# Two fused transformer blocks: product with values a step later in the last layers, gates in odd steps, third spatial sum ahead of the maximum, mask of the forgetting attention added by VectorE

## Chip, core and metric

The kernel runs on one core of one Trainium2 chip. The metric is the time of the program on the device in microseconds. Three runs of the kernel before gave 1648.83, 1653.23 and 1654.64; their median is 1653.23.

## The reference

512 tokens of width 1024, everything in float32. A first block of two layers (a convolution with memory attention, then forgetting attention with memory attention, each followed by a gated feed-forward net with a short convolution) feeds a second block of two layers, the "last layers". What the change touches is the forgetting attention and the two last layers:

```python
# forgetting attention, 12 heads of 64, block of 128 queries
logits = einsum("bqhd,bkhd->bhqk", qb, kb) * scale
logits = logits + cum_logf[:, :, q0:kend, None] - cum_logf[:, :, None, :kend]
logits = where(kpos[None, :] <= qpos[:, None], logits, -inf)
p = softmax(logits, axis=-1)
out = einsum("bhqk,bkhd->bqhd", p, vb)

# a last layer
proj = einsum('bsd,de->bse', rmsnorm(x), w_in[l])
u_a, v_a, g_a, q, k, v, g_b = split(proj)
z = einsum('hij,bcjhd->bcihd', spatial_w, layernorm(v_a)) + spatial_b
y_a = u_a * z * silu(g_a)
y_b = attention(rope(norm(q)), rope(norm(k)), v) * silu(g_b)   # 8 heads, 2 of keys and values
x = x + rmsnorm(concat([y_a, y_b]) @ w_out[l]) * post_g
```

## The kernel before

All activations stay on the chip. Each weight tile of 1024x128 is a "unit": SP loads it (raw), ScalarE rounds it to w_hi, GpSimd (POOL) subtracts for w_lo, and TensorE computes 8 tiles k of three matmuls of 512 columns each (L1886 to L1888) into one of two accumulators. VectorE scales the result out of PSUM (L1214), which frees the accumulator for the unit after the next. Every engine's program is written out by hand in its own block, in the order in which it issues; semaphores tie them together. An engine that waits holds up all that is queued behind the wait.

Attention is cut into steps that are set between the tiles of the units (the argument `before` of `unit`: a list of tile number and action). In a last layer of 22 units, `steps_in(j)` gives the steps of unit j: one every 6 tiles from unit 9 on, 18 in all for 16 blocks (a pair of heads and 128 queries each; 4 blocks make a pair of heads in full). In step i:

- TensorE computes the scores of block i into one of two pairs of banks (L2068, L2069), and, if `batch_weighed(i)` names one, the product of a batch of two blocks with the values (`weigh`, L2445).
- VectorE takes the maxima (`maxima`, L1333 to L1335), turns the probabilities of batch `batch_turned(i)` in 32x32 blocks (`turned_probs`, L1724; the single buffer pt_c must have been read by the product before), takes the reciprocals (`inverses`, L1346), and multiplies a finished pair of heads by its gate (`gated`, L1731). The product of an even batch reuses the single output bank and waits for that gate (yb_ok).
- ScalarE computes the exponentials (L801), GpSimd scales them (L662), and SP exchanges quarters of a batch by 16 DMAs (L627) ahead of the transposes.

Between these lie, in order: queries and keys with their rotation (`rope`, `q_low`, `key_norm`, `k_low`) in units 4 to 8; the layer norm of the spatial path (`add_square`, row sums L2031, normalization on ScalarE L1052); transposes to tokens (`to_tokens`, L2414) in units 16 and 17; four spatial sums (`spatial`, L2425) around units 18 and 19, each into the one bank b_mix, so that each waits until VectorE has mixed the one before (`mixed`, L1737 and L1738). After unit 21 `token_output` runs the output projection tile by tile, with the product of the last batch ahead of tile 4. In layer 0 TensorE also transposes x between the tiles of units 8 and 9 (L2400).

In the forgetting attention (24 blocks of 128 queries with 128, 256, 384 or 512 keys, between the tiles of the units that make keys and values) there is one pair of score banks (`spaced`). For each of two heads TensorE adds to the scores the gate row (L2078) and the triangle of the mask, as a bf16 identity times a bf16 mask (L2082); the maximum on VectorE is L1338, the exponentials L809, the scaling L662, the transposes L2091, the product L2108. The next block's scores wait for the exponentials of this one (at_exp).

Of the kernel before, what the change touches and what calls it, by code (L numbers as in the profile page):

```python
# [19 lines left out]
P = 128  # L20
# [16 lines left out]
QT = T // P  # L37
# [97 lines left out]
def two_blocks(nc, wstream, xT, memT, params, consts, rope, wsT, sbT, post_rows, out):  # L135
# [8 lines left out]
    with ctx:  # L144
# [52 lines left out]
        row_m = put("row_m", [P, 1], f32)  # L197
        row_t = put("row_t", [P, 1], f32)
        row_r = put("row_r", [P, 2 * QT], f32)
        ident_b = put("ident_b", [P, P], bf16)  # L200
        mask_b = put("mask_b", [P, P], bf16)
        sel = put("sel", [P, N_FOX], f32r)
        h0 = cursor[0] + (xs_at - cursor[0]) % LINE

# [312 lines left out]

        def batch_weighed(s):

            return (s - 5) // 2 if s % 2 == 1 and s >= 5 else None  # L520

        def swaps(l, batch):

# [200 lines left out]
        def _(act):  # L724
# [169 lines left out]
            high(6)  # L894
            act.wait_ge(params_in, 16)
            act.wait_ge(consts_in, 16)
            A(ident_b[:], ident, ACT.Copy).then_inc(consts_b, 1)
            A(mask_b[:], mask, ACT.Copy).then_inc(consts_b, 1)
            A(sel[:], gate_of, ACT.Copy).then_inc(consts_b, 1)
            for u in range(7, U_GLU + AHEAD):  # L900
                high(u)
# [296 lines left out]
        def _(dve):  # L1198
# [125 lines left out]
            def maxima(a, i):  # L1324
                nk = keys_of(a, i % QT)
                b = a.i0 + i
                n = 2 * (b % 2)
                dve.wait_ge(at_s, 2 * (b + 1))
                if b >= 2:
                    dve.wait_ge(at_exp, 2 * (b - 1))  # L1330
                scores_of = a.s[b % len(a.s)][:, :, 0:nk]
                if a.scale_rows:
                    own.link(V.tensor_reduce(nraw[:], scores_of, AX.X, ALU.max, negate=True))  # L1333
                    V.tensor_scalar(nmax[:, n:n + 1], nraw[:, 0:1], head_r[:, 2 * i:2 * i + 1], None, MUL)
                    V.tensor_scalar(nmax[:, n + 1:n + 2], nraw[:, 1:2], head_r[:, 2 * i + 1:2 * i + 2], None,  # L1335
                                    MUL).then_inc(at_max, 1)
                else:
                    V.tensor_reduce(nmax[:, n:n + 2], scores_of, AX.X, ALU.max, negate=True).then_inc(at_max, 1)  # L1338

            def inverses(a, i):  # L1340
# [312 lines left out]
            for l in range(2):  # L1653
# [95 lines left out]
                for j in range(IN2_UNITS):  # L1749
                    if l == 0 and j == 3:  # L1750
                        final_norm()
                    if j == 10:
                        va_sum(3)
                    if j == 19:
                        mixed(1)
                    if j == 20:
                        mixed(3)
                    for n, (_, i) in enumerate(steps_in(j)):
                        if j == 18 and n == 1:
                            mixed(0)  # L1760
                        if i < a.n:
                            maxima(a, i)
                        batch = batch_turned(i)
                        if batch is not None:
                            turned_probs(batch)
                        if j == 13:
                            invert(f"ln{l}")
                        if j == 19:
                            mixed(2)
                        if i < a.n:  # L1770
                            inverses(a, i)
                        if j == 9 and n == 0:
                            va_sum(1)
                            va_sum(2)
                        if j == 12 and n == 0:
                            for t in (2, 3):
                                add_square(f"ln{l}", t)
                        if i >= 8 and i % QT == 0:
                            gated(i // QT - 2)
                        if i == a.n + 1:  # L1780
                            for k in range(AT - 1):
                                y_low(k, gb[:, k, :])
                    if j == 4:
                        rope(0)
                    if j == 5:
                        rope(1)
                        rope(2)
                    if j == 6:
                        rope(3)
                        invert(f"qk{l}")  # L1790
                        rope(4)
                        q_low(0)
                    if j == 8:
                        k_low()
                    if j == 7:
                        key_norm()
                    if j in (10, 13, 16):
                        q_low((10, 13, 16).index(j) + 1)
                    if j == 10:
                        for t in (0, 1):  # L1800
                            centred(t)
                    if j == 11:
                        for t in (2, 3):
                            centred(t)
                        for t in (0, 1):
                            add_square(f"ln{l}", t)
                    if j == 14:
                        dve.wait_ge(cast_up, cast_no[f"ln{l}"] + 1)
                        for t in range(AT):
                            V.tensor_tensor(va[:, t, :], va[:, t, :], cast_bank(f"ln{l}")[:],  # L1810
                                            MUL).then_inc(s_norm if t < AT - 1 else cast_down, 1)
                    if j >= 20:
                        ya(j - 20)
                        dve.wait_ge(ya_ok, AT * l + j - 19)
                    dst = (qk[:, j, :] if j < 5 else vch[:] if j == 5 else va[:, j - 6, :] if j < 10
                           else gb[:, j - 10, :] if j < 14 else ua[:, j - 14, :] if j < 18 else ga[:, j % 2, :])
                    if j == 5:
                        values_scaled(u0 + j)
                    else:
                        scaled(dst, u0 + j, bank=b_s[2] if j == 2 else None)  # L1820
                ya(2)
                for t in range(2):
                    y_low(AT - 1 + t, ua[:, t, :])
                turned_probs(a.n // 2 - 1)
# [56 lines left out]
        def _(pe):  # L1881
# [176 lines left out]
            def scores(a, i):  # L2058
# [17 lines left out]
                if a.causal:  # L2076
                    for e in range(2):
                        MM(dst[:, e, 0:nk], sel[half(e), 2 * p + e:2 * p + e + 1].to_broadcast([HD, P]),  # L2078
                           a.gates[half(e), 0:nk], start=False, stop=False)

                    for e in range(2):
                        MM(dst[:, e, nk - P:nk], ident_b[:], mask_b[:], start=False, stop=True).then_inc(at_s, 1)  # L2082

            def transposes(a, i):
                b = a.i0 + i
# [231 lines left out]
            def b_step(i):  # L2317
                if i < B_BLOCKS:
# [2 lines left out]
                        pe.wait_ge(acc_free, accs_before(U_B) + Q_UNIT)  # L2321
                    if a is att_f and n == 0:
                        pe.wait_ge(f_done, 2)
                        pe.wait_ge(consts_b, 3)
                    if a is att_f and n % QT == 0:
                        pe.wait_ge(acc_free, accs_before(U_B) + K_UNIT[n // QT] + 1)
                    scores(a, n)
# [31 lines left out]
            for l in range(2):  # L2359
# [87 lines left out]
                                last.then_inc(at_o, 1)  # L2447

                def attention_step(i):
                    if i == 0:  # L2450
                        pe.wait_ge(vt_down, VT_C0 + l + 1)
                    if i < a.n:
                        if i % QT == 0:
# [10 lines left out]
                for j in range(3, IN2_UNITS):  # L2464
# [22 lines left out]
                    if j == 19:  # L2487
                        spatial(3)
                token_output(l, u0 + IN2_UNITS, a0 + IN2_UNITS, KT * (SP_YC0, SP_YC1)[l],
                             before=[(4, lambda: weigh(a.n // 2 - 1))])  # L2490

# [141 lines left out]
```

## Time and profile before

| | |
|---|---|
| median of three runs | 1653.23 us |
| the profiled execution | 1653.36 us, of it 1651.6 span |
| TensorE busy | 1605.1 us (97%), 8452 matmuls |
| VectorE busy | 883.3 us (53%) |
| ScalarE busy | 733.1 us (44%) |
| GpSimd busy | 714.2 us (43%) |
| granted TensorE clock, mean | 0.996 |
| chain that ended last | TensorE 85%, VectorE 10%, ScalarE 2%, issue 2% |

The trace is of one execution. A row of the order of time reads: start and duration in us, engine, line of the kernel, operation, written and read tensors, shape, count of merged instructions, and in brackets how long the engine had stood idle before it and what released it. PE is TensorE, DVE VectorE, ACT ScalarE, POOL GpSimd. The forgetting attention runs from 656 to 777 us, the last layer 0 from about 1200 to 1430, the last layer 1 from there to the end.

### The profile page before, as it was taken

Reading aid. Unit: us, or ns where it says so; the run is one execution under the profiler, and the core shown is the slowest. Engines: PE = TensorE matmul, PEld = TensorE weight load, DVE = VectorE, ACT = ScalarE, POOL = GpSimd, SP = SyncE. Lnnn points to the kernel's source line nnn. Section 1 sums busy time; section 2 is a strip of 40 time slices with the busy share of each in tenths; the row PEclk is TensorE's granted clock in tenths of the full one; section 3 lists DMA queues with packets and bytes.
Section 4 is the critical chain, followed back from the end, with each engine's and each line's share of the span. In section 5 each row is a group of like instructions: output and inputs, shape, how many; then the busy total and the mean of one; then the engine's idle time right before and its main releaser. Section 6 shows DMA issues by size and latency. Waiting matters only on the chain.

```text
span 1651.6 us, 23637 instructions
## 1 busy us (share of the span) xinstructions
PE 1605.1 (97%) x8452; PEld 1270.7 (77%) x8452; DVE 883.3 (53%) x1451; ACT 733.1 (44%) x1157; POOL 714.2 (43%) x406
## 2 busy tenths in 40 slices
PE   8899999999999999999999999999999999999998
PEld 7656788888888887666888888888887777887776
DVE  7887545445521124434366666611286654587654
ACT  6433544444432235444455555533335643535532
POOL 4433334444445444443444444454435542445431
PEclk9999999999999999999999999999999999999999
DMA  7212133323333332111223233333422443324441
GB/s 255 65 52 65 53 101 102 99 89 91 102 113 102 103 103 71 47 50 39 90 90 102 90 90 100 102 115 112 136 77 81 135 135 109 121 65 131 126 139 51
DMA packets 52972, 161.01 MB, mean 97 GB/s; under 512 B 8736, under 2 KB 8864, under 8 KB 52896
## 3 DMA queue, kind: packets, MB, share of 16 engines
q1 hardware_dynamic: 51744, 156.31, 30.9%
q10 hardware_dynamic: 1152, 3.67, 0.7%
q8 instruction: 49, 0.80, 0.2%
q14 instruction: 27, 0.22, 0.0%
HBM read 141.08 MB, written 2.10 MB: 87 GB/s over the span
## 4 chain that ended last, share of the span: by engine, by line
PE 85%; DVE 10%; ACT 2%; issue 2%; DMA 0%; POOL 0%; DVEq 0%; SPq 0%; ACTq 0%; POOLq 0%
PE banks L1886 23%; PE banks L1888 23%; PE banks L1887 23%; PE banks L2445 2%; PE banks L1932 2%; PE banks L1933 2%; PE banks L1934 2%; PE banks L2161 1%; PE banks L2073 1%; PE banks L2108 1%; DVE roped L1678 1%; PE banks L2091 1%; DVE chain L1497 1%; DVE pt_c L1724 1%; PE banks L2068 1%
## 5 line engine op out<-in xcount | busy, mean ns | idle before, releaser
L651 POOL TENSOR_TENSOR w_lo<-raw,w_hi 128x1024 fp32r<-128x1024 f32 x252 | 610.1, 2430 | 700.4 <-ACT w_hi L734 700.2
L1886 PE MATMUL banks<-xs_hi,w_hi 128*128 128x512 f32 (+2 forms) x1488 | 590.7, 397 | 5.1 <-DVE xs_lo L1559 1.6
L1888 PE MATMUL banks<-xs_hi,w_lo 128*128 128x512 f32 (+2 forms) x1488 | 577.5, 388 | 0.0
L1887 PE MATMUL banks<-xs_lo,w_hi 128*128 128x512 f32 (+2 forms) x1488 | 576.6, 388 | 0.0
L734 ACT ACTIVATE w_hi<-raw 128x1024 fp32r<-128x1024 f32 x255 | 263.8, 1052 | 235.8 <-PE banks L1888 204.6
L1886 PEld LDWEIGHTS banks<-xs_hi,w_hi 128*128 128x128 f32 x1488 | 280.2, 188 | 74.4 <-issue 19.0
L1888 PEld LDWEIGHTS banks<-xs_hi,w_lo 128*128 128x128 f32 x1488 | 280.0, 188 | 57.8
L1887 PEld LDWEIGHTS banks<-xs_lo,w_hi 128*128 128x128 f32 x1488 | 280.6, 189 | 52.3 <-issue 0.5
L1886 PE MATMUL banks<-hid_hi,w_hi 128*128 128x512 f32 x352 | 136.9, 389 | 0.0
L1887 PE MATMUL banks<-hid_lo,w_hi 128*128 128x512 f32 x352 | 136.9, 389 | 0.0
L1888 PE MATMUL banks<-hid_hi,w_lo 128*128 128x512 f32 x352 | 136.9, 389 | 0.0
L1410 DVE TENSOR_TENSOR x<-x,banks 128x512 f32<-128x512 f32 x16 | 11.0, 688 | 182.4 <-PE banks L1888 182.4
L1384 DVE TENSOR_TENSOR u_v<-banks,rstd 128x512 f32<-128x512 f32 x44 | 30.5, 692 | 127.5 <-PE banks L1888 127.5
L662 POOL TENSOR_SCALAR prob_c<-prob_c,rinv 128x512 f32<-128x512 f32 x64 | 53.3, 845 | 91.2 <-DVE rinv L1346 91.2
L801 ACT ACTIVATE prob_c<-banks,nmax,head_r 128x512 f32<-128x512 f32 x64 | 49.3, 774 | 89.4 <-DVE nmax L1335 89.3
L662 POOL TENSOR_SCALAR prob<-prob,rinv 128x256 f32<-128x256 f32 (+3 forms) x80 | 44.0, 563 | 88.1 <-DVE rinv L1346 87.9
L851 ACT ACTIVATE t_v<-u_v,par 128x512 f32<-128x512 f32 x44 | 35.9, 816 | 102.7 <-DVE u_v L1384 102.7
L809 ACT ACTIVATE prob<-banks,nmax 128x256 f32<-128x256 f32 (+3 forms) x80 | 39.8, 502 | 88.0 <-DVE nmax L1338 87.7
L1886 PEld LDWEIGHTS banks<-hid_hi,w_hi 128*128 128x128 f32 x352 | 66.1, 188 | 13.8
L1888 PEld LDWEIGHTS banks<-hid_hi,w_lo 128*128 128x128 f32 x352 | 66.1, 188 | 13.7
L1887 PEld LDWEIGHTS banks<-hid_lo,w_hi 128*128 128x128 f32 x352 | 66.1, 188 | 13.6
L856 ACT ACTIVATE hid_hi<-t_g 128x512 f32 x44 | 27.8, 632 | 80.6 <-DVE t_g L1397 80.6
(273 smaller groups left out, 2018.9 us busy)
## 6 DMA issues: line engine op xcount, KB each, us to landing
raw<-wstream SPq DMA_DIRECT2D x255, 512.0 KB, 3.5
swap_c<-prob_c SPq DMA_DIRECT2D x256, 64.0 KB, 2.0
x<-xT SPq DMA_DIRECT2D x4, 512.0 KB, 9.7
out<-pt SPq DMA_DIRECT2D x8, 256.0 KB, 2.0
memx<-memT SPq DMA_DIRECT2D x4, 256.0 KB, 5.1
ws_sb<-wsT ACTq DMA_DIRECT2D x2, 512.0 KB, 4.6
rope_sb<-rope ACTq DMA_DIRECT2D x2, 512.0 KB, 6.1
qk<-post_rows ACTq DMA_DIRECT2D x2, 512.0 KB, 5.0
```

The costliest lines, as they stand in the source:

```text
L651: nc.gpsimd.tensor_tensor(w_lo[s][:].rearrange("p k c -> p (k c)"), raw[s][:], w_hi[s][:].rearrange("p k c -> p (k c)").bitcast(f32), SUB) ...
L662: nc.gpsimd.tensor_scalar(p, p, rinv[:, n:n + 1], 1.0, MUL, MUL).then_inc(at_p, 1)
L734: A(w_hi[s][:].rearrange("p k c -> p (k c)"), raw[s][:], ACT.Copy).then_inc(unit_hi, 1)
L801: A(probs_of(i // 2)[:, :, 2 * (i % 2) + e, :], a.s[b % len(a.s)][:, e, :].rearrange("p (c k) -> p c k", k=P), ACT.Exp, bias=nmax[:, n:n + 1],
L809: A(prob[b % 2][:, e, 0:nk], a.s[b % len(a.s)][:, e, 0:nk], ACT.Exp, bias=nmax[:, n:n + 1], accum_out=rsum[:, n:n + 1]).then_inc(at_exp, 1)
L851: A(dst[:], src[:, 2:T + 2], ACT.Identity, scale=par[:, bass.ds(ch * 3 + (w0 + 2), 1)], bias=par[:, bass.ds(ch + b0, 1)]).then_inc(tap0, 1)
L1886: MM(dst, w_hi[slot][:, k, :], hi, start=start, stop=False)
L1887: MM(dst, w_hi[slot][:, k, :], lo, start=False, stop=False)
L1888: return MM(dst, w_lo[slot][:, k, :], hi, start=False, stop=stop)
L1932: MM(dst, hi, w_rows(w_hi, slot, half), start=start, stop=False)
L1933: MM(dst, lo, w_rows(w_hi, slot, half), start=False, stop=False)
L1934: return MM(dst, hi, w_rows(w_lo, slot, half), start=False, stop=stop)
```

## The change

- The mask is no longer multiplied in on TensorE. VectorE adds it, from the constants in float32, to the last 128 key columns of both heads' scores in PSUM, ahead of the maximum, and waits for its own add. The two bf16 copies of identity and mask, made by ScalarE at the start, go.
- `batch_weighed` gives even steps from 6 on: each product with values is one step (6 tiles) later. Batch 6, which was in step 17, stands ahead of tile 1 of the output projection; batch 7 stays ahead of tile 4.
- `gated` stands in steps 9, 13 and 17 instead of 8, 12 and 16.
- `mixed(2)` stands ahead of the maximum and the transposes of step 14 (unit 19) instead of behind them.
- TensorE waits for the turned values (vt_down) at step 1 instead of step 0.
- `q_low(0)` stands behind the scaling of unit 6 instead of ahead of it.
- `y_low(2)` stands behind `ya(2)` after the last unit instead of with y_low(0) and y_low(1) in step 17.

```diff
-            return (s - 5) // 2 if s % 2 == 1 and s >= 5 else None
+            return s // 2 - 3 if s % 2 == 0 and s >= 6 else None
...
-            A(ident_b[:], ident, ACT.Copy).then_inc(consts_b, 1)
-            A(mask_b[:], mask, ACT.Copy).then_inc(consts_b, 1)
...
                 else:
+                    if a.causal:
+                        diagonal = a.s[b % len(a.s)][:, :, nk - P:nk]
+                        own.link(V.tensor_tensor(diagonal, diagonal, mask.unsqueeze(1).to_broadcast([P, 2, P]), ADD))
                     V.tensor_reduce(nmax[:, n:n + 2], scores_of, AX.X, ALU.max, negate=True).then_inc(at_max, 1)
...
+                        if j == 19:
+                            mixed(2)
                         if i < a.n:
                             maxima(a, i)
...
-                        if j == 19:
-                            mixed(2)
                         if i < a.n:
                             inverses(a, i)
...
-                        if i >= 8 and i % QT == 0:
+                        if i >= 9 and i % QT == 1:
                             gated(i // QT - 2)
                         if i == a.n + 1:
-                            for k in range(AT - 1):
+                            for k in range(2):
                                 y_low(k, gb[:, k, :])
...
-                        q_low(0)
...
                         scaled(dst, u0 + j, bank=b_s[2] if j == 2 else None)
+                    if j == 6:
+                        q_low(0)
                 ya(2)
+                y_low(2, gb[:, 2, :])
...
                            a.gates[half(e), 0:nk], start=False, stop=False)
-
-                    for e in range(2):
-                        MM(dst[:, e, nk - P:nk], ident_b[:], mask_b[:], start=False, stop=True).then_inc(at_s, 1)
+                           a.gates[half(e), 0:nk], start=False, stop=True).then_inc(at_s, 1)
...
-                    if i == 0:
+                    if i == 1:
                         pe.wait_ge(vt_down, VT_C0 + l + 1)
...
-                             before=[(4, lambda: weigh(a.n // 2 - 1))])
+                             before=[(1, lambda: weigh(a.n // 2 - 2)), (4, lambda: weigh(a.n // 2 - 1))])
```

## Rows read from the trace of the kernel before

**Rows 1.** The page, part 1: busy us, share of the span, instructions.

```profile
PE 1605.1 (97%) x8452; PEld 1270.7 (77%) x8452; DVE 883.3 (53%) x1451; ACT 733.1 (44%) x1157; POOL 714.2 (43%) x406
```

**Rows 2.** Waits of TensorE, whole span: us in total, times, longest.

```profile
PE banks L2425 <- DVE ua L1738: 5.1, 2, 2.6
PE banks L2445 <- DVE gb L1731: 4.4, 2, 2.2
...
PE banks L2445 <- DVE pt_c L1724: 3.5, 2, 1.7
PE banks L2068 <- issue: 1.9, 1, 1.9
...
PE banks L1886 <- DVE va L1214: 1.2, 2, 0.6
...
PE banks L2068 <- DVE k_lo L1697: 0.5, 1, 0.5
```

**Rows 3.** Windows of 10 us: engines' busy time, granted clock, DMA share, GB/s.

```profile
1350.00:1360.00 10.00, 10.00 (x48) 7.39 (x47) 3.50 (x8) 5.11 (x9) 2.75 (x3) 0.89 0.36 120
1530.00:1540.00 10.00, 7.81 (x36) 5.44 (x35) 6.93 (x13) 7.18 (x14) 4.36 (x5) 0.83 0.41 100
1580.00:1590.00 10.00, 10.00 (x50) 7.15 (x47) 3.34 (x7) 3.80 (x7) 4.53 (x5) 0.83 0.34 113
```

**Rows 4.** Order of time, ScalarE, layer 0, around the first scores.

```profile
1246.08 0.60 ACT L832 ACTIVATE vtok<-banks 128x512 f32<-128x512 f32 x1
```

**Rows 5.** Order of time, TensorE, layer 0, steps 5 to 15.

```profile
1277.52 1.95 PE L2445 MATMUL banks<-pt_c,vtok 128*64 128x256 f32 x16 [1.73 <-DVE pt_c L1724]
...
1282.26 0.95 PE L2031 MATMUL banks<-cst,sq_sum 128*128 128x1 f32 x8
...
1305.34 1.95 PE L2445 MATMUL banks<-pt_c,vtok 128*64 128x256 f32 x16 [2.19 <-DVE gb L1731]
...
1309.39 0.60 PE L2414 MATMUL banks<-cst,va 128*128 128x128 f32 x4
...
1331.62 0.39 PE L2068 MATMUL banks<-k_hi,q_stack 128*128 128x512 f32 x1
...
1339.37 1.09 PE L2425 MATMUL banks<-ws_sb,va_tok 128*64 128x128 f32 x16
...
1347.55 1.09 PE L2425 MATMUL banks<-ws_sb,va_tok 128*64 128x128 f32 x16 [2.56 <-DVE ua L1738]
```

**Rows 6.** The same stretch of TensorE in layer 1: product of batch 2.

```profile
1535.48 2.77 PE L2445 MATMUL banks<-pt_c,vtok 128*64 128x256 f32 x16 [2.19 <-DVE gb L1731]
...
1541.14 0.60 PE L2414 MATMUL banks<-cst,va 128*128 128x128 f32 x4
```

**Rows 7.** Order of time, VectorE and ScalarE, layer 0.

```profile
1277.43 1.77 DVE L1238 TENSOR_TENSOR sq_sum<-sq_sum,sq_qk 128x512 f32<-128x512 f32 x2
...
1303.84 2.92 ACT L1052 ACTIVATE va<-va,par 128x512 f32<-128x512 f32 x4
...
1330.32 0.67 DVE L1731 TENSOR_TENSOR gb<-banks,gb 128x512 f32<-128x512 f32 x1
...
1336.02 0.17 DVE L1346 RECIPROCAL rinv<-rsum 128x2 f32<-128x2 f32 x1 [1.70 <-ACT prob_c L801]
```

**Rows 8.** Forgetting attention around a block of 256 keys; two VectorE groups (ns, or us).

```profile
684.42 0.29 PE L2082 MATMUL banks<-mask_b,ident_b 128*128 128x128 bf16 x2
684.54 0.39 PE L2091 MATMUL banks<-cst,prob 128*128 128x128 f32 x2
...
686.29 0.20 ACT L809 ACTIVATION_READ_ACCUMULATOR prob<-banks,nmax 128x1 f32 x1
...
686.93 0.92 PE L2073 MATMUL banks<-kf,qf 64*128 64x384 f32 x4
...
L1440 DVE TENSOR_TENSOR mem_kv<-banks,rstd_m x8: 406/412/425, 38.0 to 180.9; 128x256 f32<-128x256 f32 x8
...
L1678 DVE TENSOR_TENSOR roped<-roped,rope_sb 128x512 f32<-128x512 f32 x10 | 17.3, 1733 | 0.3
```

More of the change, by code:

```diff
@@ L199, in two_blocks @@
         row_r = put("row_r", [P, 2 * QT], f32)
-        ident_b = put("ident_b", [P, P], bf16)
-        mask_b = put("mask_b", [P, P], bf16)
         sel = put("sel", [P, N_FOX], f32r)
@@ L2078, in scores @@
                         MM(dst[:, e, 0:nk], sel[half(e), 2 * p + e:2 * p + e + 1].to_broadcast([HD, P]),
-                           a.gates[half(e), 0:nk], start=False, stop=False)
-                    for e in range(2):
-                        MM(dst[:, e, nk - P:nk], ident_b[:], mask_b[:], start=False, stop=True).then_inc(at_s, 1)
+                           a.gates[half(e), 0:nk], start=False, stop=True).then_inc(at_s, 1)
             def transposes(a, i):
@@ L2323, in b_step @@
                         pe.wait_ge(f_done, 2)
-                        pe.wait_ge(consts_b, 3)
+                        pe.wait_ge(consts_b, 1)
                     if a is att_f and n % QT == 0:
```

## The prediction

> **What bounds the kernel.** I read the page first, then TensorE's waits, the clock by windows, and last the order of time on TensorE, VectorE and ScalarE around each wait. TensorE is busy for 1605.1 of 1651.6 us [rows 1], so an edit pays only if it takes instructions off TensorE or shortens one of its waits. The waits that the change touches are few and large [rows 2]: third spatial sum 5.1 us in two, product with values behind the gate 4.4 in two, behind turned probabilities 3.5 in two, first scores 1.9 once, unit 8 of each layer 1.2 in two, first scores behind k_lo 0.5 once. In the last two layers the clock falls too: 0.89 of full speed after the spatial wait of layer 0, 0.83 after the gate wait and 0.83 after the spatial wait of layer 1 [rows 3]. That is a stay at 1.2 GHz instead of 2.4 in part of each window. Both idles of 2.56 us and one of the two of 2.19 led to it; 1.93 and 1.73 did not.
>
> **What is removed in the last layers.** (a) The wait for the turned values moves from step 0 to step 1. It held step 0 for 1.93 us: ScalarE copied vtok until 1246.68 [rows 4] and the scores began right after. k_lo, the next release, was there before TensorE came (TensorE waits for it in layer 1 only). Gain 1.93, layer 0 only; in layer 1 the same scores wait 0.5 us for k_lo [rows 2], which does not move. (b) The product of batch 0 waited 1.73 us for the transposes of its own step [rows 5]; one step later these have ended. Gain 1.73 per layer. (c) The product of batch 2 waited 2.19 us for the gate of pair 0, queued on VectorE behind a transpose [rows 5]. The gate now stands in odd steps and the product in the next even step, over 4 us later. Gain 2.19 per layer. (d) The fourth spatial sum waited 2.56 us for the third one's mixing, queued behind the maximum and the transposes of step 14 [rows 5]; now it is ahead of both. Gain 2.56 per layer. (e) q_low(0) moves behind the scaling of unit 6, which ends the 0.6 us before unit 8. I give it nothing: key_norm, k_high and k_lo follow at their old times, and the next wait (first scores on k_lo in layer 1, the turned x tiles in layer 0) grows by the same 0.6. Sum a to d: 1.93 + 2 x (1.73 + 2.19 + 2.56) = 14.9 us.
>
> (f) Clock. From the product of batch 2 to the next transposes layer 1 took 1541.14 - 1535.48 = 5.66 us, layer 0 at full clock 1309.39 - 1305.34 = 4.05 [rows 5, 6]. A fall costs 1.6 us. There are three, each behind a wait that goes: 4.8 us.
>
> **What is late next.** These are the new waits, worked out by laying the new order over the old rows.
> (g) Row sums of the layer norm. Without wait and product of batch 0, TensorE reaches them 1.73 + 1.95 less 0.08 of overlap, plus a little issue time, some 3.76 us earlier: 1282.26 - 3.76 = 1278.50. VectorE finishes the squares at 1277.43 + 1.77 = 1279.20 [rows 5, 7]. New wait 0.75 per layer.
> (h) The first tokens (1309.39) need ScalarE's normalization, which ended at 1303.84 + 2.92 = 1306.76 [rows 5, 7]. TensorE comes 1.73 + 2.19 + 1.9 (one product less by then) - 0.75 = 5.1 earlier, at 1304.3. The normalization hangs on VectorE and ScalarE; by my estimate it moves 1.9 earlier (VectorE idled about 2.5 us for the scores of block 6, and ScalarE's exponentials of that block, held by their table loads, leave 1.9 of it), so it ends at 1304.85. New wait about 0.6 per layer (0 to 2.4).
> (i) The product that stood in step 13 (1.95) is gone from there, and the gate of pair 1 (0.6 net of overlap) stands in front of the mixing of the second spatial sum. From the scores of block 13 (1331.62) the reciprocal comes after 4.40 us (1336.02), then gate 0.7, scaling 0.6, mixing 1.43: end at +7.2. TensorE is ready for the third spatial sum at 1339.37 - 1331.62 - 1.97 = +5.78 [rows 5, 7]. New wait 1.4 per layer, bounds 0.8 (the gate overlaps) to 2.0.
> Sum g to i: 2 x (0.75 + 0.6 + 1.43) = 5.6 us.
> The tail: VectorE's transposes of batch b now wait for the product of b-1 in the same step, 0.4 us behind the maximum, and are needed two steps on. Queued behind them are the reciprocal, the next scaling and POOL's probabilities; none is within 1 us of a use. The swap DMAs on SP start at their old distance from the scores (10 to 11 us of issue per batch) and land before each transpose; batch 7 lands some 1 us late for VectorE, but 5 us ahead of TensorE. The product of batch 6 in tile 1 of the output projection needs nothing late; y_low(2) is ready about 5 us before tile 2. Cost nothing; if that cover went, the 1 to 5 us would have to be used up first.
>
> **Forgetting attention.** 24 blocks lose two mask matmuls: 684.54 - 684.42 = 0.12 us to the next start [rows 8], 24 x 0.12 = 2.9. VectorE gets an add over 128x256 with a PSUM input and output. The nearest row, PSUM times SBUF at that size, takes 0.41 [rows 8]; the upper bound is the 128x512 gate product of 0.67 [rows 7]. The trace shows no such add in place at 256 columns. With 0.03 to the dependent reduction it is 0.45, and the scores are reported 0.22 earlier without the mask. The maximum ends 0.23 later. Behind it wait exponentials, reciprocal, POOL, transposes, and, as there is one score bank pair, the next block's scores. Tightest are 256 keys before 384: exponentials end 686.49 with the read at 686.29, next scores 686.93 [rows 8], 0.44 free against 0.23 + 0.12. Where POOL comes late already, 0.12 to 0.24 of the gain is given back (three blocks, 0.6), and the last block lies open on both (0.35). Net 2.9 - 1.0 = 1.9 us, bounds 0 (add of 0.67) to 3.3 (0.21 at the five outputs, no loss). The two copies removed at the start lie on ScalarE where TensorE waits for nothing of theirs; nothing.
>
> One question decides whether that price holds: VectorE's adds on roped, both inputs in SBUF, average 1.73 us at 128x512 against 0.67 for the gate product [rows 7, 8]. If the mask add were stretched alike it would cost 1 us or more. The stretched rows have two SBUF inputs, the unstretched a PSUM one; the mask add is of the second kind.
> The Trainium skill, page SBUF — State Buffer, section Who interferes with whom, says the same: a VectorE instruction with two SBUF inputs contends with a GpSimd instruction that reads SBUF, one with at most one does not. By that rule the add keeps its 0.41 and the sum below stands; were the inputs' place of no account, the sum would be that of R5.
>
> **Sum.** 14.9 + 4.8 - 5.6 + 1.9 = 16.0. The profiled execution took 1653.36 (1651.6 of span, 1.8 around it), 0.1 above the median 1653.23. 1653.36 - 16.0 = 1637.4 us.
>
> **Rivals.**
> R1, forecast, 1637.4, chance 0.54; its own range 1635 to 1640.
> R2, no new waits: VectorE and ScalarE follow as fast as TensorE. Then 14.9 + 4.8 + 1.9 = 21.6: 1631.8. For it: VectorE idles 1.7 us before many reciprocals. Against: in g and i those idles are already counted. 0.15.
> R3, clock: the new 1.4 us waits, or their sum with those before, bring the falls back. Two falls 3.2: 1640.6; three 4.8: 1642.2. For it: at 2.19 us it went both ways. Against: nothing at 1.93 or less did. 0.16.
> R4, the attention chain eats the mask's gain: add of 0.67 plus a longer link, so the four tight blocks and the last lose 0.3 each and POOL's more: 1639.4. 0.08.
> R5, slower: the mask add is stretched as the roped ones are. Extra time x per block first fills 0.1 (before 384), 0.5 (before 512) and 1.3 (before 256) and then stands on TensorE: six pairs, 6 x (3x - 1.9) from x = 1.3 on. It outweighs 16.0 at x = 1.5; at x = 1.8, as in the longest roped adds, it is 21, and the time 1658. Against: every row with a PSUM input. 0.02.
> That the reorder does not move what it says (the product still waits in its new step) is a case too: b and c stay with their clock fall, 9.4 us back, 1646.8; against it are the 4 us margins. 0.05.
>
> **Range and chances.** R1, R2, R3 and R4 hold 0.93; between 1631.5 and 1642.5 lie nearly all of them. A measurement of this kernel can tell about 0.3% (5 us) from no change: faster means under 1648.3. Faster 0.93, same 0.05, slower 0.02.
>
> **What would show it.** Right: no TensorE wait on the gate or the transposes before products with values; the first scores of layer 0 right behind the products before them; VectorE's mask add near 0.41 us; new waits of TensorE on sq_sum (0.75), va (0.6) and ua at the third spatial sum (1.4), each twice; windows at clock 1.00 throughout both layers; TensorE's wait on POOL in the attention up by under 1 us. Wrong: the wait at the third spatial sum at 2 us or more with a clock under 1.00 behind it; a mask add over 0.7 us; waits on the scores (exponentials) in the attention.

## The result and the profile after

The changed kernel takes 1638.13 us (median of 4, 1637.64 to 1638.63) against 1653.27 for the kernel before in the same session (median of 4): ratio 0.991, 95% interval 0.9896 to 0.9923. The forecast was 1637.4, from 16.0 us of gain. The profiled execution took 1638.61 with a span of 1636.8, so the span fell by 14.8 us.

The page, part 1 (busy us, share of the span, instructions), answers to [rows 1]:

```profile
PE 1599.8 (98%) x8404; PEld 1266.5 (77%) x8404; DVE 895.1 (55%) x1475; ACT 730.7 (45%) x1155; POOL 713.4 (44%) x406
```

TensorE lost 5.3 us of busy time and the span lost 14.8, so nearly two thirds of the gain is idle time. VectorE gained 24 instructions and 11.8 us, which costs the span nothing by itself.

TensorE's waits over the whole span (us in total, times, longest), which answer to [rows 2]:

```profile
PE banks L2423 <- DVE ua L1737: 2.9, 2, 1.4
...
PE banks L2032 <- DVE sq_sum L1234: 1.5, 2, 0.7
...
PE banks L2069 <- DVE k_lo L1696: 1.3, 1, 1.3
PE banks L2412 <- ACT va L1048: 1.3, 2, 0.7
...
PE banks L2398 <- DVE banks L1684: 0.4, 1, 0.4
...
PE banks L2398 <- ACT x L1073: 0.4, 1, 0.4
```

The four large rows of before have no successor: no product with values waits, neither for the gate nor for turned probabilities, and the first scores of layer 0 don't either. What was 14.9 us of waits is gone. In their place stand the third spatial sum (2.9), the row sums (1.5) and the first tokens (1.3): 5.7 where 5.6 was forecast.

The same places in order of time on TensorE, layer 0 (answers to [rows 5]; start us, us, engine, line, operation, with the idle time before it and its releaser in brackets):

```profile
1275.93 1.05 PE L2032 MATMUL banks<-cst,sq_sum 128*128 128x1 f32 x8 [0.74 <-DVE sq_sum L1234]
...
1279.34 1.95 PE L2443 MATMUL banks<-pt_c,vtok 128*64 128x256 f32 x16
...
1301.68 0.66 PE L2412 MATMUL banks<-cst,va 128*128 128x128 f32 x4 [0.60 <-ACT va L1048]
...
1305.26 1.95 PE L2443 MATMUL banks<-pt_c,vtok 128*64 128x256 f32 x16
...
1333.29 1.09 PE L2423 MATMUL banks<-ws_sb,va_tok 128*64 128x128 f32 x16 [1.44 <-DVE ua L1737]
...
1340.95 1.09 PE L2423 MATMUL banks<-ws_sb,va_tok 128*64 128x128 f32 x16
```

The new waits are 0.74, 0.60 and 1.44 us; the forecast had 0.75, 0.6 and 1.4. The fourth spatial sum (1340.95) waits no longer. The windows (length, busy times, granted clock third from the right) answer to [rows 3]:

```profile
60.00:70.00 10.00, 7.66 (x33) 5.06 (x31) 8.42 (x17) 4.23 (x12) 3.34 (x5) 0.83 0.16 52
...
1350.00:1360.00 10.00, 10.00 (x54) 7.55 (x52) 8.95 (x13) 6.81 (x11) 3.17 (x2) 1.00 0.55 148
1530.00:1540.00 10.00, 10.00 (x54) 7.45 (x53) 7.99 (x12) 8.10 (x13) 7.04 (x5) 1.00 0.61 152
1580.00:1590.00 10.00, 10.00 (x53) 7.52 (x52) 6.98 (x10) 3.20 (x5) 2.38 (x1) 1.00 0.54 157
```

Both last layers run at 2.4 GHz as long as TensorE works. One new stay at 1.2 GHz lies in 60 to 70 us, beside the first memory attention, where TensorE also waits.

Where in the span the time went is read from the first and last start of two lines of the code (times of least, median and longest in ns, then first and last start). The first line below is the scores of the forgetting attention, the second the head sums in unit 6 of both last layers (first of layer 0, last of layer 1), in the kernel before and then in the changed one:

```profile
L2073 PE MATMUL banks<-kf,qf x96: 272/481/693, 662.1 to 766.7; 64*128 64x128 f32 x24, 64*128 64x256 f32 x24, 64*128 64x384 f32 x24, 64*128 64x512 f32 x24
L2371 PE MATMUL banks<-cst,sq_qk x80: 165/251/251, 1219.8 to 1462.6; 128*128 128x2 f32 x80
```

```profile
L2074 PE MATMUL banks<-kf,qf x96: 271/482/694, 662.7 to 765.3; 64*128 64x128 f32 x24, 64*128 64x256 f32 x24, 64*128 64x384 f32 x24, 64*128 64x512 f32 x24
L2369 PE MATMUL banks<-cst,sq_qk x80: 165/251/252, 1218.7 to 1454.4; 128*128 128x2 f32 x80
```

These two lines cut every kernel of this study into three stretches: A from the first forgetting scores to the head sums of layer 0 (the attention, with a feed-forward stage that doesn't change), B from there to the head sums of layer 1 (most of layer 0), C from there to the end of the span. The table below is read in that way from each trace, which is of one execution; the last column is the median of all. The time ahead of A is left out: it differs by up to 1.2 us from one execution to the next, as the first transfers land.

```
kernel              A      B      C     median us
before            557.7  242.8  189.0   1653.3
changed           556.0  235.7  182.4   1638.1
mask_only         556.0  242.9  189.0   1651.9
values_wait_only  557.6  240.6  189.0   1651.3
mixing_only       557.6  238.7  183.1   1644.7
products_only     557.6  238.3  182.9   1643.1
mixing_back       556.1  236.7  183.5   1640.8
qlow_back         556.1  235.7  182.4   1638.1
gates_even        556.0  235.1  181.9   1637.0
mixing_early      556.0  234.2  181.0   1635.3
three_moved       556.0  233.6  180.2   1633.5
tokens_later      556.0  233.1  179.7   1632.6
mask_twice        558.9  235.7  182.5   1641.8
mask_sbuf         572.1  235.7  182.5   1654.9
```

The changed kernel gains 1.7 in A (forecast 1.9), 7.1 in B and 6.6 in C. The forecast's terms for layer 0 are 1.93 + 1.73 + 2.19 + 2.56 + one clock fall of 1.6 - 2.75 of new waits = 7.3, for layer 1 1.73 + 2.19 + 2.56 + 3.2 - 2.75 = 6.9. Some 0.6 of the 15.4 went in a later start of A (662.7 against 662.1), which belongs to no edit.

### The profile page after: what moved, and what is told of

Same layout as the page of the kernel before. It is cut to its first block, busy times and chain, and to the rows that moved or that the text cites. A ratio compares the mean times of both kernels' runs of the same rounds, so it can differ in the third digit from the quotient of the medians.

```text
span 1636.8 us, 23565 instructions
## 1 busy us (share of the span) xinstructions
PE 1599.8 (98%) x8404; PEld 1266.5 (77%) x8404; DVE 895.1 (55%) x1475; ACT 730.7 (45%) x1155; POOL 713.4 (44%) x406
## 4 chain that ended last, share of the span: by engine, by line
PE 81%; DVE 9%; SPq 3%; ACT 3%; issue 2%; DMA 1%; POOL 1%; DVEq 0%; ACTq 0%; POOLq 0%
PE banks L1887 22%; PE banks L1889 22%; PE banks L1888 22%; SPq L625 3%; PE banks L1933 2%; PE banks L1934 2%; PE banks L1935 2%; PE banks L2159 1%; PE banks L2074 1%; PE banks L2089 1%; PE banks L2106 1%; PE banks L2443 1%; DVE roped L1677 1%; DVE chain L1496 1%; ACT prob_c L799 1%
```

## The experiments

Kernels of one session share their runs of the kernel before (medians 1653.83, 1653.72, 1653.57 and 1653.47 in the four sessions).

### The parts alone, on the kernel before

**mask_only.** The forgetting attention's part alone.

```diff
-                        MM(dst[:, e, nk - P:nk], ident_b[:], mask_b[:], start=False, stop=True).then_inc(at_s, 1)
...
+                        own.link(V.tensor_tensor(diagonal, diagonal, mask.unsqueeze(1).to_broadcast([P, 2, P]), ADD))
```

> The kernel before with the forgetting attention's part alone: 48 mask matmuls go, VectorE adds the mask in PSUM. Forecast: 1.9 us less than before (0 to 3.3), about 1651.4; mask add 0.43 us, TensorE's wait for POOL in that attention up by less than 1 us, nothing changed in the last layers and their three clock falls still there. R4 (the attention's chain eats the gain): within 0.2 us of before, TensorE's waits up by as much as the matmuls saved. R5 (add stretched to 1.8 us): 21 us slower, about 1674.

Measured 1651.91, ratio 0.9988 (0.9979 to 0.9998). Stretch A took 556.0 us, 1.7 less, and B and C did not move. TensorE waited 1.3 us for POOL in that attention instead of 0.9, and for nothing else there that it had not waited for before. R4 and R5 are out.

**values_wait_only.** The wait for the turned values in step 1.

```diff
-                    if i == 0:
+                    if i == 1:
                         pe.wait_ge(vt_down, VT_C0 + l + 1)
```

> The kernel before with the wait for the turned values in step 1 instead of step 0, and nothing else. Forecast: 1.9 us less, layer 0 only, about 1651.4: the first scores of layer 0 start right behind the product before them, and layer 1 keeps its 0.5 for k_lo. Rival (k_lo or step 1 is late next): under 0.5 less.

Measured 1651.32, ratio 0.9979 (0.997 to 0.9989). B is 2.2 shorter, C unchanged, and the row of 1.9 us is gone. The size is right, but the clock did something that the forecast's reading does not allow. Everything from there on in layer 0 runs 2 us earlier and is otherwise the same; its waits of 2.19 and 2.56 us are both still there:

```profile
1303.17 2.47 PE L2445 MATMUL banks<-pt_c,vtok 128*64 128x256 f32 x16 [2.19 <-DVE gb L1731]
...
1347.00 1.09 PE L2425 MATMUL banks<-ws_sb,va_tok 128*64 128x128 f32 x16 [2.56 <-DVE ua L1738]
```

and its windows:

```profile
1300.00:1310.00 10.00, 7.81 (x38) 5.46 (x37) 5.35 (x10) 8.80 (x16) 3.27 (x5) 0.83 0.48 121
1340.00:1350.00 10.00, 7.44 (x44) 5.81 (x45) 7.17 (x11) 2.57 (x5) 2.89 (x3) 1.00 0.42 96
1350.00:1360.00 10.00, 10.00 (x52) 7.53 (x51) 5.54 (x9) 6.69 (x11) 4.25 (x4) 1.00 0.47 158
```

The fall now follows the 2.19 us (in the kernel before that stretch was at full clock: the product took 1.95 [rows 5], here 2.47), and none follows the 2.56, where before one did [rows 3]. The same two idles, 2 us earlier in time, changed places.

Whether the 2 us did this is not shown, since there is one trace of each kernel and the executions of one kernel differ by as much as the falls are worth. Two of the ten of this kernel took 1646.34 and 1647.62 us at a mean granted clock of 0.998, the other eight 1650.28 to 1652.88 at 0.994 to 0.996. Of the 52 executions of the kernel before that this study has, two took 1648.49 and 1648.83, the others 1652.01 to 1656.13. The 5 us are the size of the three falls (4.8), so these few executions may well have had none; no trace was taken of them.

**mixing_only.** The mixing of the third spatial sum ahead of the maximum.

```diff
+                        if j == 19:
+                            mixed(2)
                         if i < a.n:
                             maxima(a, i)
...
-                        if j == 19:
-                            mixed(2)
```

> The kernel before with the third spatial sum's mixing ahead of the maximum and the transposes of its step, and nothing else. By the forecast's terms: both waits of 2.56 before the fourth spatial sum go, and with them the clock falls behind them (2 x 1.6): 8.3 us less than before, about 1645.0, windows behind 1350 and 1580 at full clock, the one behind 1530 still low. If the clock falls have another cause than that wait: 5.1 less, about 1648.2, with the falls still in the windows. If something else of that step is late next: 1653.

Measured 1644.69, ratio 0.9941 (0.9925 to 0.9958). B is 4.1 shorter (2.56 + 1.6 makes 4.2). C is 5.9 shorter, where 2.56 + 1.6 is only 4.2: the fall behind the gate in layer 1, which was to stay, went too. Its wait did not:

```profile
1531.65 1.95 PE L2445 MATMUL banks<-pt_c,vtok 128*64 128x256 f32 x16 [2.19 <-DVE gb L1731]
```

and the window behind it was at full clock:

```profile
1530.00:1540.00 10.00, 8.35 (x46) 6.66 (x47) 4.51 (x9) 7.36 (x14) 5.11 (x5) 1.00 0.48 122
```

This is the same idle of 2.19 us, with 1.95 us for the product behind it instead of 2.77 in [rows 6]. Total 5.1 + 4.8 = 9.9 against 10.0 in B and C. So in this trace all three falls are gone and were worth 1.6 each, but they do not belong each to its own wait. The traced execution was the shortest of the four (1643.69 us at a mean clock of 0.999); the others took 1644.30 to 1645.28 at 0.996. In the two longest of them the fall behind the gate may have stayed, as I had expected; that is not shown.

**products_only.** The products with values one step later, on the kernel before.

```diff
-            return (s - 5) // 2 if s % 2 == 1 and s >= 5 else None
+            return s // 2 - 3 if s % 2 == 0 and s >= 6 else None
...
-                             before=[(4, lambda: weigh(a.n // 2 - 1))])
+                             before=[(1, lambda: weigh(a.n // 2 - 2)), (4, lambda: weigh(a.n // 2 - 1))])
```

> The kernel before with the products with values one step later and nothing else; gates stay in even steps, the fourth spatial sum stays behind the maximum. By the forecast's terms: the waits for transposes (2 x 1.73) and for the gate (2 x 2.19) go, and one clock fall behind the gate in layer 1 (1.6): 9.4. New: row sums 2 x 0.75, tokens 2 x 0.6, third spatial sum 2 x 0.75, and the fourth waits 2.9 in place of 2.56 (its transposes now wait for a product): 4.9. Net 4.5, about 1648.8, with clock falls behind the two fourth spatial sums left. R2 (no new waits): 1643.9. The reorder doesn't do what it says: about 1653, with products still waiting.

Measured 1643.12, ratio 0.9931 (0.9914 to 0.9947): 5.7 below what I expected, and the only one of the four times that I had wrong. The waits for the gate and for turned probabilities are gone. What I had wrong is the fourth spatial sum:

```profile
1345.18 1.09 PE L2425 MATMUL banks<-ws_sb,va_tok 128*64 128x128 f32 x16 [0.94 <-DVE ua L1738]
```

It waits 0.94 us, not 2.9. The product of batch 4 now stands in step 14, between the third sum and the fourth, and its own 1.95 us cover the wait: 2.56 + 0.4 - 1.95 = 1.0. I had moved the product and had not moved its length. That makes 3.9 in two layers. The clock is full in both layers, which makes another 3.2. With these 7.1 the expected 4.5 become 11.6; B and C are 10.6 shorter, and the 1.0 between is not explained. The new wait of 0.9 for a weight tile in this trace lies at 13.75 us, ahead of stretch A, where the start differs from one execution to the next.

The parts therefore don't add: products alone 10.7, mixing alone 9.1, mask 1.9, values 2.5, together 24.2, while the change gives 15.7 against the same 1653.8 (15.1 in its own session). The stretches of the traces show where the excess lies: the parts give 10.6 + 10.0 + 1.7 + 2.2 = 24.5 there, and the change 15.4. Of the 9.1 too many, 4.8 are the clock falls, which either of the first two takes away whole in its trace, and 3.2 are the wait of the fourth sum, which either shortens (2 x 1.62 by the products, and again in the whole 2 x 2.56 of the mixing). The last 1.1 is the price of the gates in odd steps, which only the whole change pays: in products_only the third sum waits 0.8 us, in the change 1.44 (see gates_even).

### Parts taken back from the changed kernel

**mixing_back.** The reverse of mixing_only's edit.

> The changed kernel (1638.1) with the third spatial sum's mixing put back behind the maximum and the transposes of its step. By the forecast's terms: the fourth spatial sum waits 2.56 again in each layer, and 0.4 more as its transposes now wait for a product: 2 x 2.9 = 5.8, and two clock falls of 1.6 come back: 9.0 slower, about 1647.1. If an idle of that length does not bring the falls: 1643.9 with full clock in both layers.

Measured 1640.79, ratio 0.992 (0.9903 to 0.9936), 2.7 above the changed kernel and 6.3 below what I expected. The fourth sum waits again, for 0.94 us in either layer, and B and C grow by 1.0 and 1.1. It is the same 1.0 as in products_only, and no fall comes with it. So within this change the third part is worth 2 to 3 us, not the 5.1 and two falls that the prediction wrote beside it; the credit was right for the sum only.

**qlow_back.** The first remainder of the queries back in front of the scaling of unit 6.

> The changed kernel with the first remainder of the queries back in front of the scaling of unit 6. Forecast (term e, worth nothing): within 0.3 us of the changed kernel, 1638.1: 0.6 comes back before unit 8 in each layer and 0.6 goes from the waits behind it (k_lo in layer 1, x tiles in layer 0). Rival (it is worth its 1.2): 1639.3.

Measured 1638.08, ratio 0.9905 (0.9888 to 0.9921). A, B and C are those of the changed kernel within 0.1. TensorE waits 1.1 us before unit 8 again, and k_lo holds it for 0.4 instead of 1.3. Term e is worth nothing, as forecast.

**gates_even.** The gates back in even steps.

```diff
-                        if i >= 9 and i % QT == 1:
+                        if i >= 8 and i % QT == 0:
```

> The changed kernel (1638.1) with the gates back in even steps, products still one step later. The prediction's term i put 0.6 of the third spatial sum's 1.4 down to the gate of pair 1 in front of the second mixing. If so, that wait falls to about 0.8 in both layers (the gate then stands in 1.5 us in which VectorE waits for the first spatial sum), and the time to about 1636.9. Rival: the gate in even steps is late for something else there (the product of batch 2 waits for it again, as before the change): 1638 to 1642.

Measured 1637.0, ratio 0.9902 (0.9888 to 0.9917): 1.1 faster than the change. The third spatial sum waits 0.8 us instead of 1.44. The gate in an odd step is what put 0.6 of that wait there in each layer, and nothing needed it: with the products a step later the even step is early enough. This part of the change costs 1.1 us.

### The new waits taken away

**mixing_early.** In the changed kernel VectorE idles 1.69 us before the reciprocal of block 13, and the second spatial sum ends in that time. Its mixing goes there:

```diff
-                    if j == 19:
-                        mixed(1)
...
+                        if j == 18 and n == 1:
+                            mixed(1)
                         if i < a.n:
                             inverses(a, i)
```

> The changed kernel with the second spatial sum's mixing moved ahead of the reciprocal of block 13, into 1.7 us in which VectorE waits for the exponentials; the gate of pair 1 and the scaling then stand behind it. If that gate and the reciprocal in front of the mixing are what the third spatial sum waits for (term i): its wait of 1.44 goes in both layers, 2.9 us less, about 1635.2. Rival: the reciprocal and scaling, now 0.5 and 1.4 us later, are late next (accumulator of unit 20, batch 6): under 1 us gained.

Measured 1635.25, ratio 0.9886 (0.987 to 0.9903): 2.9 less, as expected. VectorE in order of time, layer 0, of the changed kernel and then of this one:

```profile
1330.54 0.17 DVE L1345 RECIPROCAL rinv<-rsum 128x2 f32<-128x2 f32 x1 [1.69 <-ACT prob_c L799]
1330.62 0.69 DVE L1730 TENSOR_TENSOR gb<-banks,gb 128x512 f32<-128x512 f32 x1
1331.22 0.68 DVE L1210 TENSOR_TENSOR ga<-banks,rstd 128x512 f32<-128x512 f32 x1
1331.82 0.69 DVE L1736 TENSOR_TENSOR banks<-banks,sb_sb 128x512 f32<-128x512 f32 x1
```

```profile
1329.50 0.70 DVE L1736 TENSOR_TENSOR banks<-banks,sb_sb 128x512 f32<-128x512 f32 x1 [0.80 <-PE banks L2423]
1330.24 0.69 DVE L1737 TENSOR_TENSOR ua<-banks,ua 128x512 f32<-128x512 f32 x1
1330.85 0.16 DVE L1345 RECIPROCAL rinv<-rsum 128x2 f32<-128x2 f32 x1
```

The mixing starts 2.3 us earlier, and the third sum follows at 1331.65 without a wait. The reciprocal ends 0.3 later, gate and scaling 0.3 too, and none of that reaches TensorE.

**three_moved.** The same, and the row sums and the first tokens each one group of three matmuls later on TensorE.

```diff
-                        before.append((2, lambda: stat(f"ln{l}")))
+                        before.append((3, lambda: stat(f"ln{l}")))
...
-                        before += [(1, lambda: to_tokens(0)), (7, lambda: to_tokens(1))]
+                        before += [(2, lambda: to_tokens(0)), (7, lambda: to_tokens(1))]
```

> The changed kernel with all three new waits taken away at once: the row sums and the first tokens one group of three matmuls (about 1.15 us) later on TensorE, and the mixing ahead of the reciprocal as in mixing_early. If terms g, h and i are each worth what the trace of the changed kernel shows (1.5, 1.3 and 2.9): 5.7 us less, about 1632.4, near the sum of rival R2. If what they delay is late next: between 1634 and 1637, with new waits behind.

Measured 1633.46, ratio 0.9878 (0.9861 to 0.9894), 1.1 above what the first theory gave. The row sums no longer wait, the first tokens wait as long as before:

```profile
1300.64 0.65 PE L2412 MATMUL banks<-cst,va 128*128 128x128 f32 x4 [0.61 <-ACT va L1048]
```

Two things were wrong. A group of three is 0.68 us, since one matmul follows the last after 0.227 us; I had taken their own 0.39. And the normalization did not move with TensorE: the 0.7 us that the row sums no longer cost came back in front of the tokens, less the 0.68 of the move.

**tokens_later.** The tokens one more group later (3 instead of 2 in the second edit above).

> three_moved (1633.5) with the first tokens one more group of three matmuls later. A group takes 0.68 us on TensorE (0.227 from matmul to matmul). If the normalization that they wait for hangs on the chain through VectorE and ScalarE from block 6 on and not on TensorE, the 0.61 left in each layer goes: 1.2 less, about 1632.3. If the normalization moves with TensorE, the tokens still wait 0.6 and the time is that of three_moved.

Measured 1632.56, ratio 0.9877 (0.986 to 0.9894). The wait for va is gone from the list, B and C are 0.5 shorter each. So the normalization hangs on the chain through VectorE and ScalarE, and the move is free. This version is 5.6 us faster than the change, and the fastest of the study.

### The price of the mask add

**mask_twice.** The mask is added twice in PSUM.

> The changed kernel with the mask added twice in PSUM, one add behind the other (the scores come out the same, as masked ones stay masked): 0.43 + 0.03 more per block on VectorE. By the chain that the forecast took (free per block: 0.1 before 384 keys, 0.5 before 512, 1.3 before 256, and the last block open): 6 x 0.36 for the blocks before 384 and 0.5 for the last, 2.7 us slower, about 1640.8. R4 in full (every block open): 24 x 0.46 = 11 slower, 1649. All hidden: 1638.1.

Measured 1641.76, ratio 0.993 (0.9914 to 0.9947), 3.6 above the changed kernel; stretch A is 2.9 longer against 2.7 expected. TensorE waits 1.6 us for exponentials where it waited none in that attention, and 2.2 for POOL instead of 1.3. The free time of 0.1 to 1.3 per block that the forecast worked with holds in the sum: eleven us of VectorE's work (24 x 0.46) cost three. The single blocks were not compared.

**mask_sbuf.** One more add of 128x256 behind the mask add, with both inputs and the output in SBUF.

```diff
+        spare = put("spare", [P, 2, P], f32)
...
+                        own.link(V.tensor_tensor(spare[:], ident.unsqueeze(1).to_broadcast([P, 2, P]),
+                                               mask.unsqueeze(1).to_broadcast([P, 2, P]), ADD))
```

> The changed kernel with one more VectorE add of the same 128x256 size behind the mask add, with both inputs and the output in SBUF (its result is not used). It measures what R5 rested on: by the roped rows against the gate product it should be stretched beside POOL, to about 0.9 to 1.1 us where the add with a PSUM input takes 0.43. Then the chain gets 0.9 to 1.1 more per block: 6 x (0.8 + 0.4) and more, 7 to 12 us slower, 1645 to 1650. If the place of the inputs is of no account: 0.43 each, and the time of mask_twice, about 1640.8.

Measured 1654.86, ratio 1.0007 (0.9997 to 1.0016): 16.7 above the changed kernel, more than I expected. The two adds in the lines of the trace (durations of least, median and longest in ns), the mask add first, and the group of the second with its mean:

```profile
L1337 DVE TENSOR_TENSOR banks<-banks,cst x24: 420/432/433, 663.4 to 780.7; 128x256 f32<-128x256 f32 x24
L1338 DVE TENSOR_TENSOR spare<-cst x24: 424/425/2567, 663.9 to 781.2; 128x256 f32<-128x256 f32 x24
```

```profile
L1338 DVE TENSOR_TENSOR spare<-cst 128x256 f32<-128x256 f32 x24 | 23.5, 978 | 0.8
```

The mean of 0.98 us is what I expected, but no add takes it: 16 take 0.42 and 8 take 1.28 to 2.57. Each of the 8 began while POOL was forming the low part of a weight tile. VectorE and POOL in order of time:

```profile
663.87 0.43 DVE L1338 TENSOR_TENSOR spare<-cst 128x256 f32<-128x256 f32 x1
...
663.95 2.60 POOL L650 TENSOR_TENSOR w_lo<-raw,w_hi 128x1024 fp32r<-128x1024 f32 x1 [1.04 <-ACT w_hi L733]
...
686.35 2.39 POOL L650 TENSOR_TENSOR w_lo<-raw,w_hi 128x1024 fp32r<-128x1024 f32 x1 [1.25 <-ACT w_hi L733]
...
686.45 2.57 DVE L1338 TENSOR_TENSOR spare<-cst 128x256 f32<-128x256 f32 x1
```

POOL began at 686.35 and VectorE at 686.45; POOL's work ended at 688.74 and the add at 689.02. All eight ended some 0.28 behind POOL's. Where VectorE was first, at 663.87, its add took 0.43 and POOL's operation 2.60 instead of 2.39. The one that comes second is held until the other has ended. A delay of 2 us in single blocks is dearer than 0.5 in each, because it exceeds the free time of every block: TensorE's wait for exponentials there was 9.0 us, its longest 2.5, and two windows (750 to 760 and 780 to 790) fell to 0.83.

The longest of these waits stands twice in this one trace, in front of the same line and shape. Behind the first the scores took 0.92 us, at full clock, and behind the second 1.55, at 1.2 GHz:

```profile
690.85 0.92 PE L2077 MATMUL banks<-kf,qf 64*128 64x384 f32 x4 [2.49 <-ACT prob L808]
...
751.48 1.55 PE L2077 MATMUL banks<-kf,qf 64*128 64x384 f32 x4 [2.49 <-ACT prob L808]
```

## Why the prediction was right, step by step

**Terms a to d.** The old waits (1.93, 3.5, 4.4, 5.1) went to the last tenth. As a price list of the edits they are wrong, as products_only and mixing_back showed: the prediction gave d its 2.56 per layer, while b and c already cover 1.62 of it by putting the product in that step. The sum is not touched by that, since all old waits go and all new ones are counted.

**Term e.** Nothing, and the next waits took it over: k_lo 1.3 instead of 0.5, x tiles 0.8 in two instead of 0.2, for 1.2 before unit 8. qlow_back confirms it.

**Term f.** The size was right, the mechanism only half. Three falls went and each was worth 1.6: in mixing_only B and C give 10.0 for 5.1 of waits, 4.9 more. "Each behind a wait that goes" was wrong: in the trace of values_wait_only one wait of 2.56 has no fall behind it, and in that of mixing_only a fall is missing whose wait stayed. That all three went here was likely, since the large waits all went, but it did not follow from those three pairs. And since a few executions of one kernel take 5 us less than the rest, the 4.8 is what the change takes off most executions and not off each. The number of falls was right by more luck than the term admits. "Nothing at 1.93 or less did" is refuted by the changed kernel itself: a fall lies at 60 to 70 us, where its longest wait is 1.71. The wait is as long in the kernel before, at full clock, and from the scores behind it to those two steps on (62.05 to 73.25 before, 62.44 to 73.82 after) the fall costs 0.2 us. R3 was thus better founded than I gave it credit for; it did not happen in the layers.

**Terms g to i.** 0.74, 0.60 to 0.7 and 1.44 measured against 0.75, 0.6 and 1.4. In h my reason was right, and it is shown: the normalization hangs on VectorE and ScalarE, as three_moved and tokens_later tell. In i the gate's share of 0.6 is shown by gates_even, the rest by mixing_early. R2 (no new waits, 1631.8) is what tokens_later nearly reaches (1632.6) by taking them away.

**The tail.** Nothing was late, as forecast: no wait stands before the products of batches 6 and 7 in the output projection.

**The mask.** 1.7 in stretch A against 1.9. The group of the add in the changed kernel:

```profile
L1336 DVE TENSOR_TENSOR banks<-banks,cst 128x256 f32<-128x256 f32 x24 | 10.4, 432 | 25.4 <-PE banks L2079 25.3
```

0.432 us against 0.41 assumed, from the multiplication of the same size in [rows 8]. R5 asked whether it would be stretched as the roped adds are. Some of the 24 mask adds ran while POOL formed a weight's low part and took 0.43 all the same:

```profile
674.67 2.36 POOL L649 TENSOR_TENSOR w_lo<-raw,w_hi 128x1024 fp32r<-128x1024 f32 x1
...
675.19 0.43 DVE L1336 TENSOR_TENSOR banks<-banks,cst 128x256 f32<-128x256 f32 x1 [1.14 <-PE banks L2079]
```

With both inputs in SBUF the same size takes up to 2.57 there. The output differs between the two adds as well (PSUM here, SBUF there), but that is not what decides: the second half of the mixing, with one input in PSUM and its output in SBUF, keeps its 0.69 us in the middle of POOL's work.

```profile
1332.13 2.35 POOL L649 TENSOR_TENSOR w_lo<-raw,w_hi 128x1024 fp32r<-128x1024 f32 x1
...
1332.55 0.69 DVE L1737 TENSOR_TENSOR ua<-banks,ua 128x512 f32<-128x512 f32 x1
```

So the split by inputs on which R5 hung is shown.
The Trainium skill, page SBUF — State Buffer, section Who interferes with whom, calls the pair of ports that VectorE shares with GpSimd an exclusive lock and says that "Issue order, not op shape, decides who blocks." By that rule the trace agrees: 2.57 us behind POOL, 0.43 ahead of it.

What R5 took for a stretch was a misreading of a mean, though. In the kernel before, none of the ten roped adds takes the 1.73 us of [rows 8]: four take 0.69, and six, which began while POOL formed a low part, 2.10 to 2.70, each ending 0.55 behind POOL's.

```profile
L1678 DVE TENSOR_TENSOR roped<-roped,rope_sb x10: 691/2110/2698, 1210.2 to 1467.0; 128x512 f32<-128x512 f32 x10
```

```profile
1214.98 2.41 POOL L651 TENSOR_TENSOR w_lo<-raw,w_hi 128x1024 fp32r<-128x1024 f32 x1 [3.03 <-ACT w_hi L734]
...
1215.24 2.70 DVE L1678 TENSOR_TENSOR roped<-roped,rope_sb 128x512 f32<-128x512 f32 x1
...
1220.10 0.69 DVE L1678 TENSOR_TENSOR roped<-roped,rope_sb 128x512 f32<-128x512 f32 x1
...
1220.42 2.61 POOL L651 TENSOR_TENSOR w_lo<-raw,w_hi 128x1024 fp32r<-128x1024 f32 x1 [3.02 <-ACT w_hi L734]
```

R5's sum, which gave every block the same extra time, was therefore of the wrong kind.

**The sum.** Forecast 14.9 + 4.8 - 5.6 + 1.9 = 16.0. Measured 14.9 + 4.9 - 5.7 - 0.2 (term e) + 1.7 = 15.6 by the parts, 15.4 in A, B and C, 14.8 in the span with its later start, and 15.1 between the medians. The 0.7 between 1637.4 and 1638.1 is of the size of these small terms.

## What to carry to other kernels

When a step is moved, move its length with it: a product of 1.95 us that leaves one step is cover for a wait in the next, and edits that cover the same wait are not worth the sum of what each is worth alone. Then look where the engine that releases the late one idles itself; a small piece of work that fits into such a gap (here 1.4 us of mixing in 1.69) is worth its whole wait, and a stall of 0.6 at a start that hangs on another chain is removed by starting later. And place no VectorE instruction with two SBUF inputs in a chain with little slack while GpSimd does long work; read the longest time of a group beside its mean.

## What the runs showed of the hardware that I had not expected

- An instruction of VectorE with two SBUF inputs is not slowed beside GpSimd, it waits for the end of GpSimd's instruction (0.42 us or 1.28 to 2.57, nothing between). The roped group's mean of 1.73 [rows 8], which I took as a stretch, is such a mixture: 0.69 us four times and 2.10 to 2.70 six times.
- TensorE's clock fell to 1.2 GHz behind idles of 1.71, 1.99, 2.19, 2.49 and 2.56 us in some places and not behind 2.19, 2.49 and 2.56 in others; in mask_twice it also fell at 86 us, behind idles of 0.91 and 0.55. What decides is not settled by these runs; only that the length of the last idle alone does not, as the two waits of 2.49 in mask_sbuf show within one execution.
- What a fall costs was 1.6 us in the last layers in all cases that could be priced, where TensorE is dense, and 0.2 at 60 to 70 us, where it waits for others anyway.
